# The causal mask of the second layer's attention: added by VectorE in the banks instead of multiplied in by TensorE

## The reference

```
s = einsum('bqgrd,bkgd->bgrqk', q, k) * scale      # k: ks or kw
s = where(kpos <= qpos, s, -1e30)                  # causal
e = exp(s - max(s)); p = e / sum(e)
o = einsum('bgrqk,bkgd->bqgrd', p, v)              # v: vs or vw
y = o_c * gate0 + o_s * gate1 + o_w * gate2        # o_c: compressed branch
```

## Time and profile before

| | us |
|---|---|
| three runs, median | 1517.88 |
| lowest and highest | 1517.81, 1520.85 |
| the profiled execution | 1517.54 |
| its span, first to last instruction | 1515.7 |
| TensorE, products, busy | 1461.7 (96%) |
| VectorE busy | 720.3 (48%) |
| ScalarE busy | 719.9 (47%) |
| GpSimd busy | 686.9 (45%) |

### The profile page before, as it was taken

How to read it: one execution, slowest core, us unless ns; L and a number is a source line. 1 busy time by engine, 2 the same in 40 slices (tenths; PEclk the granted TensorE clock), 3 DMA queues, 4 the chain that set the end, 5 groups by cost and what they waited for, 6 DMA issues and landing times.

```text
span 1515.7 us, 23491 instructions
## 1 busy us (share of the span) xinstructions
PE 1461.7 (96%) x7566; PEld 1215.8 (80%) x7566; DVE 720.3 (48%) x1256; ACT 719.9 (47%) x1308; POOL 686.9 (45%) x982
## 2 busy tenths in 40 slices
PE   6999999899999999999999999999999999999998
PEld 5877767788888888887978787878888888888886
DVE  5477772644444400246466767674644343410053
ACT  5245555654444423357365656463744444423262
POOL 4634436465656555363420202111456555555452
PEclk9999999999999999999999999999999999999999
DMA  5321113232222322242410101010232222232221
GB/s 211 114 68 57 56 43 111 84 111 97 96 98 92 102 97 98 70 141 84 162 55 4 56 14 43 14 42 28 64 134 94 98 96 97 97 99 96 97 97 56
DMA packets 37563, 127.80 MB, mean 84 GB/s; under 512 B 6144, under 2 KB 6912, under 8 KB 37248
## 3 DMA queue, kind: packets, MB, share of 16 engines
q1 hardware_dynamic: 32256, 117.45, 23.1%
q10 hardware_dynamic: 5248, 9.55, 1.8%
HBM read 124.90 MB, written 2.10 MB: 84 GB/s over the span
## 4 chain that ended last, share of the span: by engine, by line
PE 57%; issue 16%; POOL 16%; DVE 5%; ACT 4%; POOLq 0%; ACTq 0%; DVEq 0%
PE banks_a L1215 21%; POOL w_lo L297 16%; PE banks_b L1225 9%; PE banks_a L1225 8%; PE banks_a L1628 4%; PE banks_b L1215 4%; PE banks_a L1192 4%; PE banks_b L1600 2%; PE banks_b L1380 1%; DVE nm L951 1%; PE banks_a L1399 1%; ACT w_hi L361 1%; PE banks_a L1519 1%; ACT y L364 1%; PE banks_b L1603 0%
## 5 line engine op out<-in xcount | busy, mean ns | idle before, releaser
L297 POOL TENSOR_TENSOR w_lo<-w_raw,w_hi 128x256 fp32r<-128x256 f32 x864 | 657.3, 794 | 764.2 <-ACT w_hi L361 763.9
L361 ACT ACTIVATE w_hi<-w_raw 128x1024 fp32r<-128x1024 f32 x216 | 228.5, 1061 | 278.0 <-PE banks_b L1225 132.6
L1215 PE MATMUL banks_a<-nT_hi,w_hi 128*128 128x512 f32 (+1 forms) x968 | 343.9, 377 | 0.0
L1215 PE MATMUL banks_a<-nT_lo,w_hi 128*128 128x512 f32 (+1 forms) x968 | 342.7, 375 | 1.0 <-DVE nT_lo L804 1.0
L1215 PE MATMUL banks_a<-nT_hi,w_lo 128*128 128x512 f32 (+1 forms) x968 | 341.5, 374 | 0.0
L1215 PEld LDWEIGHTS banks_a<-nT_lo,w_hi 128*128 128x128 f32 x968 | 174.0, 189 | 32.4 <-DVE nT_lo L804 1.2
L1215 PEld LDWEIGHTS banks_a<-nT_hi,w_hi 128*128 128x128 f32 x968 | 174.2, 189 | 31.5
L1215 PEld LDWEIGHTS banks_a<-nT_hi,w_lo 128*128 128x128 f32 x968 | 173.3, 188 | 32.0
L857 DVE SCALAR_TENSOR_TENSOR y<-banks_a,conv,y 128x511 f32<-128x511 f32 x88 | 66.0, 750 | 219.7 <-ACT y L466 219.2
L466 ACT ACTIVATE y<-banks_a,conv 128x512 f32<-128x512 f32 x88 | 68.6, 779 | 208.9 <-PE banks_a L1215 208.8
L704 ACT ACTIVATE gp<-banks_b,nm 128x128 f32<-128x128 f32 (+3 forms) x128 | 67.6, 528 | 49.1 <-DVE nm L951 43.4
(11 more groups left out here) (256 smaller groups left out, 2392.0 us busy)
## 6 DMA issues: line engine op xcount, KB each, us to landing
w_raw<-in_w SPq DMA_DIRECT2D x216, 512.0 KB, 3.2
g_pre<-in_gains ACTq DMA_DIRECT2D x6, 512.0 KB, 4.5
x<-in_x SPq DMA_DIRECT2D x4, 512.0 KB, 9.4
g_post<-in_gains ACTq DMA_DIRECT2D x4, 512.0 KB, 6.5
out<-x SPq DMA_DIRECT2D x4, 512.0 KB, 2.6
pe_raw<-in_pT ACTq DMA_DIRECT2D x2, 512.0 KB, 4.8
w1k<-in_w ACTq DMA_DIRECT2D x1, 1024.0 KB, 4.7
w1v<-in_w ACTq DMA_DIRECT2D x1, 1024.0 KB, 6.8
```

What stands on the lines that cost most here:

```text
L297: pool.tensor_tensor(w_lo[slot][:, cols], w_raw[k % RAW][:, cols], w_hi[slot][:, cols].bitcast(F32), ALU.subtract).then_inc(S["w_lo_done"], 1)
L361: act.activation(w_hi[u % RING][:, :], w_raw[u % RAW][:, :], ACT.Copy).then_inc(S["w_hi_done"], 1)
L1215: m = pe.matmul(bank[:, cols], w[:, k * P:(k + 1) * P], r[:, k, cols], start=(k, pas) == (0, 0), stop=(k, pas) == (KT - 1, 2))
```

## The change

VectorE adds the table `causal_b`, the same for both branches, to the last 128 columns of the two banks of a step, in one instruction, and waits for it before the maximum. The two products with the identity are dropped, the product with the keys' low part closes the accumulation, and the semaphore that they raised is raised by that product, twice a step as before. The loop's count of links grows by one a step.

```diff
                 def gmaxima(h, k):
+                    n, b = (ORDER[k] + 1) * P, 2 * (k % 2)
+                    dve.wait_ge(S["gscores_done"], 2 * step(h, k) + 2)
+                    diagonal = banks_b[:, b:b + 2, n - P:n]
+                    link(dve.tensor_tensor(diagonal, diagonal, causal_b[:, :].unsqueeze(1).broadcast_to([P, 2, P]),
+                                           ALU.add))
                     maxima(ORDER[k], 2 * (k % 2), "gscores_done", "gnegmax_done", step(h, k))
...
-            with chain.loop(1, GROUPS, 3 * 3 + 4 + 1 + 1 + 2 + TT + 4 * 4) as g:
+            with chain.loop(1, GROUPS, 3 * 3 + 4 + 1 + 1 + 2 + TT + 4 * 4 + 4 * TT) as g:
...
                         for K in (Kh, Kl):
-                            pe.matmul(B[2 * (k % 2) + c][:, 0:n], Q[h][:, tok(qt)], K[:, c, 0:n],
-                                      start=K is Kh, stop=False)
-                    for c in range(2):
-                        pe.matmul(B[2 * (k % 2) + c][:, n - P:n], ident_b[:, :], causal_b[:, :], start=False,
-                                  stop=True).then_inc(S["gscores_done"], 1)
+                            m = pe.matmul(B[2 * (k % 2) + c][:, 0:n], Q[h][:, tok(qt)], K[:, c, 0:n],
+                                          start=K is Kh, stop=K is Kl)
+                        m.then_inc(S["gscores_done"], 1)
```

## The result

The changed kernel takes 1533.41 us (median of four runs, 1532.93 to 1537.37), the kernel before 1518.28 beside it (1517.81 to 1520.85). The ratio is 1.0095 with an interval of 1.0081 to 1.0109: 14.4 us slower (12.3 to 16.5). Forecast were +18.9 us and 1536.4 us, with a range of 1528 to 1543. The direction and the loop that sets the time were right. One term of the sum, the gap behind the addition, was 0.1 us too large in 48 places.

A forecast was written before the change was run, and what follows sets the result against it. It took each head's loop of waits over TensorE, VectorE and ScalarE as the bound. Three loop groups at 5.3 us gave 15.8, the first group 3.1: +18.9 on 1517.5, so 1536.4 us, range 1528 to 1543.

The forecast's parts named there:

- the gap behind the addition: VectorE, between the new addition and the maximum: one more gap, 0.13 us in three loop groups, 0.03 in the first.
- The head is a loop over three engines: Second layer's attention: a head's 10.28 us is a chain of waits over TensorE, VectorE and ScalarE, not TensorE's full order.
- the half to k3: Loop head, from transposes of step k1 (512 keys) to those of k3 (384 keys): 4.96 us, forecast to grow 0.80.
- The pairs take 0.12 us each, and scores are complete 0.13 earlier: TensorE: 64 dropped mask product pairs free 8 us of its order; in the loop only the 0.13 us counts.
- the half to k1: Loop head, from transposes of step k3 (384 keys) to those of k1 (512 keys): 5.32 us, forecast to grow 0.42.
- The addition, 0.42 us: VectorE, between scores and maximum: each of 64 additions of 128x256 on banks takes 0.42 us.
- VectorE's queue brings the copy of k1 0.25 us later: Loop heads: VectorE's late queue starts its copy of k1's transposes 1.45 us after them, not 1.20, raising the k3 half.
- the start of a loop's group: First head of each loop group: turn of k1 +0.95 us, then way to k3's transposes +0.65; 1.60 together.
- the cheap gap: Rival, loop groups: extra gap is nothing, 0.03 us everywhere; +14.2 us, 1531.7 us; chance 0.16 together with a cheap addition.
- TensorE-bound: Rival: TensorE's order is the bound, 64 x 0.12 us goes off and additions hide in VectorE's idle time; 1509.5 us; chance 0.07.
- one for one: Rival: additions are paid and the products' time won back equally, leaving 1517.5 us; chance 0.04.
- the dear addition: Rival, VectorE: each addition takes 0.69 us, its queue becomes the bound or nearly so; +32 us, 1549.5 us; chance 0.05.

The follow-up runs named there:

- e1: Kernel before with the second layer's causal mask products dropped and nothing in their place: ratio 0.9982, -2.7 us against the kernel before.
- e7: Changed kernel with VectorE adding the mask only in steps k0 and k2, TensorE keeping its products in k1 and k3: ratio 1.0007, +1.1 us against the kernel before.
- e3: Kernel before with ScalarE's copies of k0's and k2's transposes moved ahead of the exponentials of k1 and k3: ratio 0.9970, -4.6 us.
- e4: Changed kernel with ScalarE's copies of k0's and k2's transposes ahead of the exponentials of k1 and k3: ratio 1.0024, +3.6 us against the kernel before.
- e9: Kernel before with VectorE adding the mask in k0 alone, and ScalarE's k0 and k2 copies ahead of the k1 and k3 exponentials: ratio 0.9958, -6.4 us.
- e5: Changed kernel with one more wait, for a long-fired semaphore, between VectorE's addition and its maximum: ratio 1.0132, +20.0 us against the kernel before.
- e2: Changed kernel with the mask products put back beside VectorE's additions: ratio 1.0101, +15.3 us against the kernel before.
- e6: Changed kernel with the addition over the first branch alone, 128x128 in place of 128x256: ratio 1.0055, +8.3 us against the kernel before.

## Why the prediction was right or wrong

- *The head is a loop over three engines, not TensorE's order.* Right, and shown: e1 gains 2.7 us where the order would have given 8, e7 leaves the head at 10.27 us, and e3 and e4 gain from an order of ScalarE alone. One thing was read too simply: in the half to k3 TensorE's order was as long as the chain (without the products it stays 4.95 us and TensorE gets a pause of 0.24, e1; with them and a shorter chain it stays 4.96, e3), so the two bounded together there. It did not matter for a change that lengthens the chain.
- *The pairs take 0.12 us each, and scores are complete 0.13 earlier.* Right: e9's half to k3 is 0.14 shorter by one pair, and in the changed kernel the addition of k1 starts 1.84 us after k3's transposes, where the maximum had started 2.01 after them. Only the half to k1 used it.
- *The addition, 0.42 us.* Right, 0.433.
- *The new gap, 0.13 us in the loop's groups.* Wrong, and the whole of the miss: it is 0.03. The step took the gap between copy and maximum as what a pair of waits costs. It is what the calculation of a wait's value costs; that calculation moved ahead of the addition and was not doubled, and e5, which puts one behind it, gets a gap back. The half to k1 therefore grew by 0.29, not 0.42.
- *VectorE's queue brings the copy of k1 0.25 us later.* Mis-sized by the same gap: in the changed kernel the copy starts 1.24 us after the transposes (878.50 to 879.74), 0.04 later than before. The half to k3 grew by 0.51, not 0.80. By the same term the start of a loop's group cost less than forecast: its way to k1's transposes 0.81 (35.61 to 36.42) for 0.95, its half to k3 0.46 (5.90 to 6.36) for 0.65.
- *Sum.* With 0.03 everywhere the prediction itself had worked out 3.7 us for a group and 14.2 in all, as a rival with the first group's rows for it; measured are 3.7 and 14.4. There the Trainium skill (VectorE: DVE Perf Modes, "The DRAIN you can't avoid") was named: a semaphore between two VectorE instructions costs nothing extra. The trace of the changed kernel agrees (0.03), and e5 in its first group (0.04). In a loop whose wait values are worked out, e5's 0.19 disagrees, and there the measurement decides. The forecast read the number of the rows rightly and took the wrong cause for it. The measured +14.4 us lies beside the rival's 14.2 and its interval does not reach the forecast's +18.9. The stated range holds the time with room to spare because its lower end was drawn down for the cheap gap. The forecast's own 1533 to 1541 holds it by 0.4 us alone, and that is chance.
- *Rivals.* TensorE-bound (1509.5) and one for one (1517.5) are refuted by the time itself, and by e1 and e2; the dear addition by its 0.433.

What stays open: how a sequencer instruction of 46 ns lengthens the gap by 0.10 us, and one of 40 and one of 21 ns by 0.16. The rows give their durations and their place, not what fills the rest of the gap. That e4's first heads gained by the rounding's place is read from its trace and was not run by itself.

## What to carry to other kernels

An engine that is busy 96% of the time can still be waiting: follow one turn of the loop in the order of time and see which pauses are missing from the chain, then ask of each instruction taken off or put in whether it stands in that chain. Here the same addition costs 0.46 us in two steps of a head and nothing in the other two, and the products taken off were worth 0.12 us a pair only in a half where TensorE had no pause. Before pricing a gap between two instructions, find out what fills it: look for the sequencer's own rows beside the wait.

## What the runs showed of the hardware

A wait for a semaphore long fired adds nothing on VectorE when its value is a constant (gap 0.04 us in e5's first group) or already at hand (0.03 in the changed kernel's loop). It adds 0.10 to 0.16 us when its value is worked out behind the instruction just ended (a gap of 0.13 in the kernel before, 0.19 in e5). An addition in place in the banks with a bfloat16 operand takes 0.433 us for 256 columns over two banks, the operand spread over both, and 0.299 for 128 columns in one bank (e6). That is 0.009 more than a VectorE instruction of the same width that reads a bank and writes elsewhere (0.424 for the addition, 0.29 for the copy).
